# Moving the pooling mixer's running sums and means from VectorE to GpSimd in a two-block transformer kernel

## The reference

```python
y = _rms(h, norm_mix_g[i]); z = y @ w_in[i]
za, zb, zc, zd = jnp.split(z, split_at, axis=-1)
oa = _mixer_sgu(za, ...); ob = _mixer_shortconv(zb, ...)
oc = _mixer_conformer(zc, ...); od = _mixer_pool(zd, pool_w[i], pool_scale[i])
h = h + jnp.concatenate([oa, ob, oc, od], axis=-1) @ w_out[i]
```

## Time and profile before

| | before |
|---|---|
| runs, us | 2143.59 median of 3 (2142.22 to 2144.16) |
| profiled execution, own time / span, us | 2144.04 / 2141.8 |
| TensorE (PE) busy | 2122.5 us, 99% of the span |
| VectorE (DVE) busy | 1202.4 us, 56% |
| ScalarE (ACT) busy | 896.2 us, 42% |
| GpSimd (POOL) busy | 21.2 us, 1% |
| mean granted TensorE clock | 0.997 |

### The profile page before, as it was taken

How to read it: one execution, slowest core, us unless ns; L and a number is a source line. 1 busy time by engine, 2 the same in 40 slices (tenths; PEclk the granted TensorE clock), 3 DMA queues, 4 the chain that set the end, 5 groups by cost and what they waited for, 6 DMA issues and landing times.

```text
span 2141.8 us, 25969 instructions
## 1 busy us (share of the span) xinstructions
PE 2122.5 (99%) x11183; PEld 1824.3 (85%) x11183; DVE 1202.4 (56%) x1189; ACT 896.2 (42%) x845; POOL 21.2 (1%) x40
## 2 busy tenths in 40 slices
PE   9999999999999999999999999999999999999998
PEld 8798989798888888888999988888888888888887
DVE  5475554565555455545789855454445444454565
ACT  5443443444344433444444444333333433344443
POOL 2000000000000000000000000000000000000000
PEclk9999999999999999999999999999999999999999
DMA  8654455454555556565665556555555555655563
GB/s 243 204 161 161 162 169 177 158 177 159 195 196 192 184 194 196 193 239 178 202 192 164 176 179 197 184 192 191 189 192 194 184 190 196 197 186 187 185 208 118
DMA packets 206257, 398.42 MB, mean 186 GB/s; under 512 B 11154, under 2 KB 19594, under 8 KB 205888
## 3 DMA queue, kind: packets, MB, share of 16 engines
q1 hardware_dynamic: 202864, 387.64, 54.9%
q0 software_dynamic: 2528, 8.00, 1.3%
q10 hardware_dynamic: 752, 1.12, 0.1%
HBM read 394.62 MB, written 2.12 MB: 185 GB/s over the span
## 4 chain that ended last, share of the span: by engine, by line
PE 93%; DVE 5%; ACT 1%; issue 0%; DMA 0%; ACTq 0%
PE psA L456 30%; PE psA L458 30%; PE psA L457 30%; DVE CA L1382 1%; DVE lo L1184 1%; PE psB L554 1%; DMA raw<-in_w_in_dram 0%; PE psB L661 0%; PE psB L646 0%; PE psB L597 0%; PE psA L772 0%; PE psB L662 0%; ACT hi L801 0%; PE psB L633 0%; PE psB L634 0%
## 5 line engine op out<-in xcount | busy, mean ns | idle before, releaser
L1184 DVE TENSOR_TENSOR lo<-raw,hi 128x2048 fp32r<-128x2048 f32 x369 | 837.3, 2272 | 682.8 <-ACT hi L801 680.8
L801 ACT ACTIVATE hi<-raw 128x2048 fp32r<-128x2048 f32 x369 | 699.1, 1899 | 696.2 <-PE psA L458 651.8
L456 PE MATMUL psA<-hi,XH 128*128 128x512 f32 x1632 | 639.8, 392 | 0.0
L458 PE MATMUL psA<-hi,XL 128*128 128x512 f32 x1632 | 634.9, 389 | 0.0
L457 PE MATMUL psA<-lo,XH 128*128 128x512 f32 x1632 | 634.8, 389 | 0.0
L456 PEld LDWEIGHTS psA<-hi,XH 128*128 128x128 f32 x1632 | 307.3, 188 | 63.8 <-issue 0.4
L458 PEld LDWEIGHTS psA<-hi,XL 128*128 128x128 f32 x1632 | 307.1, 188 | 63.9
L457 PEld LDWEIGHTS psA<-lo,XH 128*128 128x128 f32 x1632 | 307.4, 188 | 61.6
L456 PE MATMUL psA<-XH,hi 128*128 128x256 f32 x1104 | 314.6, 285 | 1.2 <-DVE lo L1224 1.2
L457 PE MATMUL psA<-XL,hi 128*128 128x256 f32 x1104 | 312.3, 283 | 0.0
L458 PE MATMUL psA<-XH,lo 128*128 128x256 f32 x1104 | 312.3, 283 | 0.0
(11 more groups left out here) (342 smaller groups left out, 1015.2 us busy)
## 6 DMA issues: line engine op xcount, KB each, us to landing
raw<-in_w_in_dram SPq DMA_DIRECT2D x159, 1024.0 KB, 5.0
raw<-in_w_gate_dram SPq DMA_DIRECT2D x44, 1024.0 KB, 5.2
raw<-in_w_up_dram SPq DMA_DIRECT2D x44, 1024.0 KB, 5.2
raw<-in_w_down_dram SPq DMA_DIRECT2D x44, 1024.0 KB, 5.0
raw<-in_w_out_dram SPq DMA_DIRECT2D x32, 1024.0 KB, 5.0
raw<-in_w_branch_dram SPq DMA_DIRECT2D x16, 1024.0 KB, 5.0
raw<-in_w_ple_gate_dram SPq DMA_DIRECT2D x16, 1024.0 KB, 5.0
raw<-in_w_in_dram SPq DMA_DIRECT2D x16, 512.0 KB, 4.7
```

Source lines behind the costliest of these rows:

```text
L456: e.matmul(dst, A2[0], B2[0], start=first, stop=False, skip_group_check=True)
L458: return e.matmul(dst, A2[1], B2[0], start=False, stop=last, skip_group_check=True)
L801: e.activation(hi[u % H][:, 0:m], raw[u % R][:, 0:m], ACT.Copy).then_inc(hi_made, 1)
L1184: e.tensor_tensor(lo[u % R][:, 0:m], raw[u % R][:, 0:m], hi[u % H][:, 0:m].bitcast(F32), ALU.subtract).then_inc(lo_made, 1)
```

## The change

`pool_sums` and `pool_means` leave VectorE's program. One `pool_sums` stands in GpSimd's, behind its DMA issues. The sums of 4 and 16 go into a P2 laid over `LG` instead of over `B[:, 1:3]`, with three groups instead of four (the sums of 4 of group 0 are not made in either version). The result goes to `B[:, 1]` instead of `B[:, 3]`, so the wait for `mix_high` is gone; a wait for `sgu_v_made` is there because `LG` must have been read. VectorE's fused multiply and subtract becomes two instructions on GpSimd.

```diff
-        P2 = B[:, 1:3, :].rearrange("p a b -> p (a b)")[:, 0:1088].rearrange("p (c n) -> p c n", c=4)
+        P2 = LG[:, :, :].rearrange("p a b -> p (a b)")[:, 0:816].rearrange("p (c n) -> p c n", c=3)
...
         def gpsimd_program(e):
+            def pool_sums():
+                w4 = c4(B[:, 1, :])
+                finish(e.memset(P1[:, :, 0:16], 0.0))
+                e.wait_ge(sgu_v_made, 1)
+                finish(e.memset(P2[:, :, 0:16], 0.0))
+                e.wait_ge(bank_dve, freed(("zd", 0)))
+                finish(e.tensor_tensor(P1[:, :, 16:272], PA[:, :, 16:272], PA[:, :, 15:271], ALU.add))
+                finish(e.tensor_tensor(P2[:, :, 16:272], P1[:, 1:4, 16:272], P1[:, 1:4, 14:270], ALU.add))
+                finish(e.tensor_tensor(P1[:, 2:4, 16:272], P2[:, 1:3, 16:272], P2[:, 1:3, 12:268], ALU.add))
+                finish(e.tensor_tensor(P2[:, 2, 16:272], P1[:, 3, 16:272], P1[:, 3, 8:264], ALU.add))
+                e.wait_ge(fc_landed, 16)
+                for g, (S, n) in enumerate(((P1[:, 0, :], 2), (P2[:, 0, :], 4), (P1[:, 2, :], 8), (P2[:, 2, :], 16))):
+                    finish(e.tensor_tensor(S[:, 16:32], S[:, 16:32], FC[:, 16 * g:16 * g + 16], ALU.mult))
+                    finish(e.tensor_scalar(S[:, 16:272], S[:, 16:272], 1.0 / n, None, ALU.mult))
+                    x = e.tensor_tensor(w4[:, g, :], S[:, 16:272], PA[:, g, 16:272], ALU.subtract)
+                x.then_inc(pool_ready, 1)
...
                         A["sgu_w_2"][0].rearrange("h t s -> t h s")).then_inc(sw_landed, 16)
+            pool_sums()
...
                 if u == 197:
-                    ps, w4 = c4(psB[:, 1, :]), c4(B[:, 3, :])
+                    ps, w4 = c4(psB[:, 1, :]), c4(B[:, 1, :])
...
                 if u == 194:
                     part_low(c4(B[:, 3, :]), 0, 0.5, 1)
-                    pool_sums()
-                if u == 195:
-                    pool_means()
```

More of the change, by code:

```diff
@@ L252, in build_hybrid @@
         bank_act, bank_dve = sem("bank_act"), sem("bank_dve")
-        act_step, dve_step = sem("act_step"), sem("dve_step")
+        act_step, dve_step, pool_step = sem("act_step"), sem("dve_step"), sem("pool_step")
         x_landed = [sem(f"x_landed{i}") for i in range(4)]
@@ L407, in gpsimd_program, with finish @@
         def gpsimd_program(e):
+            steps = [0]
+            def finish(x):
+                steps[0] += 1
+                x.then_inc(pool_step, 1)
+                e.wait_ge(pool_step, steps[0])
+            def pool_sums():
[14 more added lines that the diff above has]
+                x.then_inc(pool_ready, 1)
             e.wait_ge(unit_done, 1)
@@ L1399, in part_low @@
                                        op1=ALU.subtract).then_inc(mix_low, 1)
[L1401 to L1418, removed]
             def side(u):
```

## The result

The changed kernel takes 2151.1 us (median of 6 runs, 2148.49 to 2152.25) against 2143.34 us before (2142.22 to 2144.16): ratio 1.0036, 95% interval 1.0026 to 1.0046. It is slower by 7.8 us where 8.4 were forecast (2152.0 against 2143.59). The profiled execution has a span of 2148.5 us against 2141.8, and 2150.74 us of its own time against 2144.04.

What follows compares the result with a forecast made beforehand. TensorE, busy 99% of the span, was taken as the bound, with VectorE as busy from 1140 to 1170 us. Delay 9.3, less gain 1.4, plus clock 0.5, gave 2152.0 us (0.39% slower), range 2142.0 to 2157.0.

Steps and rivals of the forecast that it cites:

- Exclusion of reads: From 1145 us, GpSimd's SBUF reads and VectorE's two-operand instructions take turns; GpSimd's whole 9.3 us delays VectorE.
- The size of D: VectorE's lateness at the last tap, set to GpSimd's priced time for 16 instructions: 9.3 us, bounds 7.06 and 15.7.
- a partial exclusion: Case of 2 to 5.7 us of VectorE delay by GpSimd's reads, ending at 2144 to 2148 us; chance 0.10.
- The prediction's own sign of failure: The prediction fails if GpSimd's 16 instructions together take far from 9 us, or VectorE keeps durations and spacing meanwhile.
- My lower bound of 7.06: Least time for GpSimd's 16 instructions, priced at VectorE's speed for the same sizes: 7.06 us.
- All of it ahead of the last tap: GpSimd's 16 instructions fit between VectorE's over 30 from 1145 to 1168.5 us, so all 9.3 us land before the last tap.
- Where TensorE stalls: First at unit 195's lo for delay beyond 4.2 us of cover, then at the channel sum (line 695) for the rest.
- The gain: VectorE's removed 5.66 us of work ends TensorE's wait for the means at line 745, winning 1.4 us at most.
- hesitations: Small later TensorE delays that the removed VectorE work would also save, allowed at 0.1 us.
- The clock: TensorE's clock falls from 2.4 to 1.2 GHz after some 2.2 us standing still; 0.5 us taken, bounds 0 and 1.1.
- Side by side: Rival: GpSimd reads without holding VectorE up beyond its cover, so 1.4 us are won, 2142.2 us; chance 0.30.
- GpSimd kept out: Rival: GpSimd stands still until VectorE first waits, TensorE waits 10.5 us at line 745, 2152.8 us; chance 0.08.

Runs made afterwards that it cites:

- e1_buffers: Kernel before, with VectorE still making sums and means but in the new buffers and without the wait for mix_high; 2142.01 us, ratio 0.9995.
- e2_no_work: Changed kernel with the 16 instructions of sums and means left out on every engine; 2140.26 us, ratio 0.9989 to before.
- e4_extra: Kernel before, VectorE's work kept, plus 16 GpSimd instructions of the change's sizes whose results go nowhere; 2149.87 us, ratio 1.0031.
- e5_after_taps: Changed kernel with GpSimd's work started only when the convolution's 124 taps are made; 2157.18 us, ratio 1.007 to before.
- e3_writes: Changed kernel with the 16 instructions replaced by 16 GpSimd memsets that write LG and read nothing; 2140.8 us, ratio 0.9993 to before.
- e6_one_input: Changed kernel with the 16 instructions replaced by 16 GpSimd multiplications by one factor, one operand read from SBUF; 2146.77 us, ratio 1.0018 to before.
- e7_sums_only: Changed kernel with only the four sums on GpSimd, corrections and means on VectorE at u = 195; 2147.85 us, ratio 1.0023 to before.
- v1_later: Kernel before, with the pooling product and what ScalarE and VectorE make of it one unit later, 198; 2143.9 us, ratio 1.0003.
- e8_filler: Changed kernel with 32 further matmuls in front of TensorE's wait for the last tap; 2147.51 us, ratio 1.0025 to before.
- v2_overlap: Changed kernel with GpSimd's work behind the 124th tap and the pooling product two units later, 199; 2147.11 us, ratio 1.002 to before.

## Why the prediction was right, step by step

- **Exclusion of reads** was the disputed term and it holds in kind, but not for the whole of GpSimd's time. e1_buffers and e2_no_work clear the buffers and the order, e4_extra puts the loss on GpSimd's load alone, e5_after_taps ties it to overlap in time, and e3_writes leaves only instructions that read. The Trainium skill, SBUF — State Buffer, "Who interferes with whom", says that a VectorE instruction with two SBUF inputs contends with a GpSimd one that reads SBUF and not with one that only writes; both halves show here (+6.65 and -0.01 us at the last tap). It also says that the loser is blocked for the whole instruction. GpSimd behind a `lo` agrees (2.77 us for the multiplication above), and VectorE behind GpSimd does not. In the changed kernel single taps of 0.47 us take 1.69 beside a sum of 1.52 us and 0.97 beside a subtraction of 0.75; in e6_one_input they take 0.61 beside a multiplication of 0.85, and over 26 us of GpSimd's work cost VectorE 3.5.
- **The size of D** was 9.3 us and is 6.8. It is the term furthest off, and it lies between the prediction's two cases (a partial exclusion up to 5.7 us, the full one from 7.06). Two errors are in it. GpSimd's own time was priced too low: by the rows above the twelve small instructions take 4 x (0.85 + 0.72 + 0.22) = 7.2 us alone, and the sums some 5.3 (1.52, 1.11 and 0.81, and an estimated 1.9 for the first by their steps of 0.4 per 256 columns), 12.5 in all. The prediction's own sign of failure, 16 instructions that together take far from 9 us, so came about. But I let all of that time exclude VectorE, and only a part of it does: 1.6 ns per column of a two-tensor instruction (e7_sums_only), 0.6 ns of a multiplication (e6_one_input). With (2560 + 4 x 272) x 1.6 + 1024 x 0.6 this gives 6.5 us, close to the 6.8. The two prices are taken from e7_sums_only and e6_one_input, so only the twelve small instructions test them. My lower bound of 7.06 was above the truth, since it rested on the same assumption. The estimate beside the sum is off by 0.1: 4672 columns at the quoted 4497 ns for 2048 are 10.3 us and not 10.4.
- **All of it ahead of the last tap**: right. GpSimd was done at 1166.3 us, the last tap at 1175.6.
- **Where TensorE stalls**: right in kind. I named a stall at unit 195 for the delay beyond 4.2 us and the rest at the channel sum; the trace has 1.45 us there, 0.20 at unit 194, and 4.90 at the sum.
- **The gain** was 1.4 us and is 1.9. The 1.31 us of the wait was right; what I called hesitations was worth 0.6 instead of 0.1, half of it at the product and half at a `lo` of out2. The second half fits v1_later, where VectorE is short at such a `lo`.
- **The clock** was 0.5 us, with an upper bound of 1.1, and cost 1.46 in the profiled execution (1.45 by e8_filler) and 2.75 in e7_sums_only. e7_sums_only shows the bound itself too low. It was taken from the time of the fall, and nothing ties the way back to that. Nor do the 2.2 us of standing still hold elsewhere: in v2_overlap the clock fell behind a stall of 1.76 us.
- So the sum was 9.3 - 1.4 + 0.5 = 8.4 and the stage measured 6.8 - 1.9 + 1.5 = 6.4; the medians differ by 7.8. The sign and the mechanism were right. The number was luck in part: D was 2.5 us too high, the gain 0.5 and the clock 1.0 too low, which leaves the sum 2.0 us above the stage, and the medians happen to lie 1.4 us above the stage as well.
- **The rivals.** Side by side is excluded. GpSimd kept out is excluded: it got its turn behind single taps, and between two `lo` tiles in e5_after_taps, where three of its sums were done before VectorE first ran out of work. A long instruction of VectorE only makes it wait longer (0.28 against 2.27 us for 16 columns). GpSimd's busy time was to grow to 30 us and is 41.1; waits for its turn count as busy.

Open: which part of an instruction GpSimd holds, above all in a one-operand instruction, whose cost per column is lower for VectorE and higher for itself, and why the clock's way back took 3.0 us after TensorE resumed in one profile and 5.8 in the other.

## What to carry to other kernels

Ask of an instruction moved to GpSimd not only whether its result is in time, but which VectorE instructions with two SBUF operands run beside it, and what waits for the last of those. Price the exclusion by the columns that GpSimd reads and by its operands (here 1.6 ns per column with two and 0.6 with one), and put the work where VectorE is idle. That it is free where VectorE reads PSUM is shown in one place only (e6_one_input, 0.85 us), and no run tests it on purpose. A short wait at the end of a saturated stretch shows where the shortage comes due and not how much there is to win: v1_later removed it and won nothing. Add the clock to any stall of TensorE of some microseconds; here it added a fifth to two thirds of the delay.

## What was not expected of the hardware

- GpSimd's multiplication by one factor of 256 columns takes 0.85 us, longer than its subtraction of two tensors of that size (0.72), though it reads half as much, and the second holds VectorE up more.
- 16 dependent memsets of 512 to 1024 columns took GpSimd 10.98 us beside VectorE without any effect on it.
- A single stall of 4.3 us (e7_sums_only) cost 2.75 us of clock and one of 4.9 us (the changed kernel) 1.46. Behind a stall of 1.76 us (v2_overlap) the clock fell, and behind one of 1.45 (the changed kernel, 1164.78) it stayed at 1.00.
- Up to 4 us of the span's differences between executions lie ahead of 1140 us, in parts that no kernel here changes.
